# A fused inference step on one core: where finished attention rows are turned, where remainders are formed, and products of constants on TensorE

## The chip, the core and the metric

The kernel runs on one core of one Trainium2 chip. The metric is device microseconds for one execution. Engines are named as in the profile: PE is TensorE, DVE is VectorE, ACT is ScalarE, POOL is GpSimd, SP is SyncE. All of them run at the same time and meet only at semaphores.

## The reference

One layer of a diffusion backbone on 128 context rows and 512 latent rows of width 1024. Cut to what matters here:

```python
sh1, sc1, g1, sh2, sc2, g2 = split(silu(cond) @ w_ada + b_ada, 6)      # two conditions
h = rms_norm(x, norm1_w) * (1 + sc1) + sh1
q, k, v, gu, gv = split(h @ w_in)
q, k = rms_norm per head (8 heads x 64)
a  = attend(q, k, v)      # context: 128 keys; latent: grid neighbourhood + 256 cached keys,
                          # scores + bias, mask, softmax, p @ v
sg = gelu(gu) * (w_s @ layer_norm(gelu(gv)) + b_s)                      # 4 groups x 128
x = x + g1 * (concat(a, sg) @ w_out)
h2 = rms_norm(x, norm2_w) * (1 + sc2) + sh2
x = x + g2 * moe(h2)      # 16 experts, top 1 of 4 groups, top 2 in it
```

Results are y_prompt, y_sample, new_k and new_v, all in fp32.

## The kernel before

The rows are five tiles of 128: tile 0 is context, tiles 1 to 4 are latent. Wherever fp32 accuracy is needed from fast products, a matrix is held as a rounded part in fp32r (hi) and the remainder (lo, "rest"); `three` makes the three products hi·hi, hi·lo, lo·hi.

The stages run in this order: the first modulation (two of six vectors), input projection, spatial gating, attention, output projection with the second norm and the router, then a software pipeline over blocks of 128 gathered rows and an expert's weights, and a gather of the results. All programs are written out by hand, one for each engine, and each engine follows its own program strictly in order.

**Attention** is a list of 40 steps n = (tile, head), eight heads for each tile. At step n PE's program is: scores of step n+1 (`scores`, L1367 for context, L1371 and L1373 for latent); perhaps one part of the second modulation (`ada_part`, L1354); the turn of the probabilities of step n (`prob_T`, L1390, one to five 128x128 transposes into banks 4 and 5); and probabilities times values of step n-1 (`values`, L1412, into bank 6). DVE's `largest` finds the row maximum (L1007 and L1008 for context; L1012, L1016, L1018 for latent, where L1012 adds the bias `bm` in SBUF to the scores in a bank). ACT's `softmax` takes the exponentials, then `copy_pT` (ACT L690, DVE L1028) fetches turned probabilities.

**The second modulation**: two groups of eight parts, at steps 2 to 9 and 20 to 27; each part is four concurrent products of 32x512 outputs into bank 7, with weights that SP streams into a ring of four slots. After a group, `ada_group` on DVE adds the bias from `norms`, and waits for all 14 pieces of the attention bias.

**Finished rows**: once a tile's eight heads are done, DVE's `normalise` (L1042) writes the rows to `o_row`. Two steps later, inside `prob_T`, `att_T` turns them by four transposes (L1419) into bank 4, which is also the bank of the turned probabilities. ACT rounds them (`copy_aT`, L695), DVE forms the rest (`rest_aT`, L984), and PE goes on only after that:

```python
if n >= 2 and steps[n - 2][1] == HEADS - 1:
    att_T(steps[n - 2][0])
    pe.wait_ge(aT_lo_ready, steps[n - 2][0] + 1)
```

**The gating rows** are rounded by ACT (`round_sg`) at steps 2 to 5, and DVE forms their rests (`rest_sg`, L971, L974, L976) at steps 3 to 6, with both inputs in SBUF.

**The attention bias** is made by POOL. After the gating's products it loads `slab`, clears `norms`, issues ten small transfers, and runs 14 additions of 128x512 in SBUF (L521). `largest` of tile 1 waits for 4 of them, of tiles 2 and 3 for 10, of tile 4 for 14.

The output projection starts when all rests are there; its first five tiles of products are L1263 to L1265. Its weights are split by ACT (L622) and DVE (L859) at steps 36 to 40 and behind the loop.

Of the kernel before, what the change touches and what calls it, by code (L numbers as in the profile page):

```python
# [12 lines left out]
ACT = mybir.ActivationFunctionType  # L13
# [39 lines left out]
def build(nc, t_in, t_out):  # L53
# [4 lines left out]
    with ctx:  # L58
# [67 lines left out]

        po, po_r = sb_both("po", 2 * D)
        pT = [po[:, s * 640:(s + 1) * 640].rearrange("p (j n) -> p j n", j=5) for s in range(2)]
        o_row = po[:, 1280:1280 + AW]

        hgT_hi, hgT_lo = [[a.rearrange("p (k n) -> p k n", k=KD) for a in ab] for ab in (
# [3 lines left out]
        rs, rs_r = sb_both("rs", 4 * 512)  # L136
        raw = [rs[:, s * 512:(s + 1) * 512] for s in range(2)]
        sq = [rs[:, (2 + s) * 512:(3 + s) * 512] for s in range(2)]
        y_sb = rs[:, 0:D]
        hidT_hi, hidT_lo = [rs_r[:, D + i * DE:D + (i + 1) * DE].rearrange("p (k n) -> p k n", k=2) for i in range(2)]  # L140
        wr_sb = sb("wr_sb", [P, KD, EXPERTS])
# [157 lines left out]

        ada_first = (2, 20)
        ada_at = {first + k: (g, k) for g, first in enumerate(ada_first) for k in range(KD)}
        ada_ends = {first + KD - 1: g for g, first in enumerate(ada_first)}

# [285 lines left out]
        def _(act):  # L591
# [101 lines left out]
            def copy_aT(t):  # L693
                act.wait_ge(aT_done, t + 1)
                nc.scalar.activation(cat_r[:, 0:4, t * P:(t + 1) * P],  # L695
                                     banks[4][:].rearrange("p (j n) -> p j n", n=P), ACT.Copy).then_inc(aT_copied, 1)

            def round_sg(j):
                if j == 0:
                    act.wait_ge(sgu_out, TILES)  # L700
                row = catT[:, 4 + j, :]
                if j < 3:
                    nc.scalar.activation(rs_r[:, j * TOK:(j + 1) * TOK], row, ACT.Copy).then_inc(sg_hi_ready, 1)
                else:
                    nc.scalar.activation(sg_hi(j, 0), row[:, 0:P], ACT.Copy)
                    nc.scalar.activation(hu_r[:, 56 * P:60 * P], row[:, P:], ACT.Copy).then_inc(sg_hi_ready, 1)

            for n in range(len(steps) + 2):
                if n < len(steps):
                    softmax(n)  # L710
                if 1 <= n <= len(steps):
                    copy_pT(n - 1)
                if n in (2, 3, 4, 5):
                    round_sg(n - 2)
                if 36 <= n < 40:
                    split_hi(("out", 0), n - 36, wout_hi)
                if n >= 2 and steps[n - 2][1] == HEADS - 1:
                    copy_aT(steps[n - 2][0])

            for piece in range(4):  # L720
                split_hi(("out", 1), piece, wout_hi)
# [102 lines left out]
        def _(dve):  # L824
# [143 lines left out]
            def rest_sg(j):  # L968
                dve.wait_ge(sg_hi_ready, j + 1)
                if j < 3:  # L970
                    V.tensor_tensor(cat_r[:, 4 + j, :], catT[:, 4 + j, :], rs_r[:, j * TOK:(j + 1) * TOK].bitcast(F32),  # L971
                                    ALU.subtract).then_inc(sg_lo_ready, 1)
                else:
                    V.tensor_tensor(cat_r[:, 7, 0:P], catT[:, 7, 0:P], sg_hi(3, 0).bitcast(F32),  # L974
                                    ALU.subtract).then_inc(sg_lo_ready, 1)
                    V.tensor_tensor(cat_r[:, 7, P:], catT[:, 7, P:], hu_r[:, 56 * P:60 * P].bitcast(F32),  # L976
                                    ALU.subtract).then_inc(sg_lo_ready, 1)

            def rest_aT(t):
                if t == 0:  # L980
                    dve.wait_ge(bias_ready, 14)
                dve.wait_ge(aT_copied, t + 1)
                ts = slice(t * P, (t + 1) * P)
                V.tensor_tensor(att_lo[:, :, ts], banks[4][:].rearrange("p (j n) -> p j n", n=P),  # L984
                                cat_r[:, 0:4, ts].bitcast(F32), ALU.subtract).then_inc(aT_lo_ready, 1)

            def ada_group(g):
# [43 lines left out]
            def normalise(t):  # L1031
                dve.wait_ge(exp_done, HEADS * (t + 1))
                if t:
                    dve.wait_ge(act_step, HEADS * t)
                    link(V.tensor_tensor(rsum, sums[:, t % 2, :, 0], sums[:, t % 2, :, 1], ALU.add))
                    link(V.reciprocal(rsum, rsum))
                else:
                    link(V.reciprocal(rsum, sums[:, 0, :, 1]))
                dve.wait_ge(pv_done, HEADS * (t + 1))
                if t:  # L1040
                    dve.wait_ge(aT_done, t)
                V.tensor_tensor(o_row.rearrange("p (h d) -> p h d", h=HEADS),  # L1042
                                banks[6][:].rearrange("p (h d) -> p h d", h=HEADS),
                                rsum.unsqueeze(2).to_broadcast((P, HEADS, HD)), ALU.mult).then_inc(o_ready, 1)

            for n in range(len(steps) + 2):
                if n < len(steps):
                    largest(n)
                if 1 <= n <= len(steps):
                    copy_pT(n - 1)  # L1050
                if n - 1 in ada_ends:
                    ada_group(ada_ends[n - 1])
                if n >= 2 and steps[n - 2][1] == HEADS - 1:
                    normalise(steps[n - 2][0])
                    rest_aT(steps[n - 2][0])
                if n in (3, 4, 5, 6):
                    rest_sg(n - 3)
                if 37 <= n < 41:
                    split_lo(("out", 0), n - 37, (wout_hi, n - 36), wout_lo)

            for piece in range(4):
                split_lo(("out", 1), piece, (wout_hi, 5 + piece), wout_lo)
            dve.wait_ge(g1_in, 32)
# [189 lines left out]
        def _(pe):  # L1253
            T = nc.tensor

            def arrived(key):
                slot = slot_of[key]
                pe.wait_ge(ring_in[slot], 16 * nth_of[key])
                return ring[slot]

            def three(out, lhs, rhs, start, stop):

                T.matmul(out, lhs[0], rhs[0], start=start, stop=False)  # L1263
                T.matmul(out, lhs[0], rhs[1], start=False, stop=False)  # L1264
                return T.matmul(out, lhs[1], rhs[0], start=False, stop=stop)  # L1265
# [76 lines left out]
            for t in range(TILES):  # L1342
                if t >= 2:
                    pe.wait_ge(sgu_out, t - 1)
                for g in range(GROUPS):
                    ins = T.matmul(banks[4 + t % 2][:, g * P:(g + 1) * P], vv[:, t, g * P:(g + 1) * P],
                                   wsT[:, g * P:(g + 1) * P], start=True, stop=True)
                ins.then_inc(sgu_done, 1)
            def ada_part(g, k):
                if k == 0 and g:  # L1350
                    pe.wait_ge(rows_ready, g)
                for q in range(4):
                    w = arrived(("ada", 4 + 4 * g + q))
                    ins = T.matmul(banks[7][32 * q:32 * (q + 1), :], silT[:, k, :], w[:, k, :], start=(k == 0),  # L1354
                                   stop=(k == KD - 1))
                if k == KD - 1:
                    ins.then_inc(ada_done, 1)
# [18 lines left out]
            def prob_T(n):  # L1376
                t, h = steps[n]
                pe.wait_ge(exp_done, n + 1)
                if t:
                    pe.wait_ge(act_step, n - HEADS + 1)  # L1380
                if n >= 1:
                    pe.wait_ge(pT_act, n)
                    if dve_copies(n - 1):
                        pe.wait_ge(pT_dve, dve_copies(n - 1))
                if n >= 2 and steps[n - 2][1] == HEADS - 1:
                    att_T(steps[n - 2][0])
                    pe.wait_ge(aT_lo_ready, steps[n - 2][0] + 1)
                for j in range(key_tiles(t)):
                    bank, at_ = (4, j) if j < 3 else (5, j - 3)
                    ins = T.transpose(banks[bank][:, at_ * P:(at_ + 1) * P], probs[n % 2][:, j * P:(j + 1) * P], ident[:])  # L1390
                ins.then_inc(pT_done, 1)
# [23 lines left out]

            def att_T(t):
                pe.wait_ge(o_ready, t + 1)
                for j in range(4):
                    ins = T.transpose(banks[4][:, j * P:(j + 1) * P], o_row[:, j * P:(j + 1) * P], ident[:])  # L1419
                ins.then_inc(aT_done, 1)  # L1420

            pe.wait_ge(cache_in, 64)
# [2 lines left out]
            for n in range(len(steps)):  # L1425
                if n + 1 < len(steps):
                    scores(n + 1)
                if n in ada_at:
                    ada_part(*ada_at[n])
                prob_T(n)  # L1430
                if n:
                    values(n - 1)
            values(len(steps) - 1)
            att_T(TILES - 1)

            pe.wait_ge(exp_done, len(steps))
            pe.wait_ge(aT_lo_ready, TILES)
# [176 lines left out]
```

## Time and profile before

| | us |
|---|---|
| three executions | 817.24, 819.72, 830.25 (median 819.72) |
| the profiled execution | 820.98 |
| its span, first to last instruction | 818.8 |
| PE busy / DVE busy / ACT busy / POOL busy | 640.1 / 436.9 / 309.8 / 146.6 |
| mean granted clock of TensorE | 0.812 |

In a timeline each row is a merged run of like instructions: its start, its length, how many (x), and in brackets how long the engine had been idle and which instruction released it.

### The profile page before, as it was taken

The numbers are of one execution on the slowest core, as the hardware profiler recorded it, in microseconds if no ns is written. First come the engines' busy times: TensorE is split into PE (matmuls) and PEld (weight loads), VectorE is DVE, ScalarE is ACT, GpSimd is POOL, SyncE is SP. The second block draws the span as 40 slices with busy tenths as digits, with TensorE's granted clock in tenths as the row PEclk, the third lists the DMA queues.
The fourth block names the chain that finished last, engine by engine and source line by source line (L and its number), as shares of the span: only waits on it lengthen the run. The fifth ranks groups of instructions, "written<-read, shape, count | busy, mean of one in ns | idle before, by whom it ended". The sixth has DMA issues, their size and how long they took to land. (4 is left out here: it accounts for less than half of the span.)

```text
span 818.8 us, 8534 instructions
## 1 busy us (share of the span) xinstructions
PE 640.1 (78%) x2932; PEld 501.1 (61%) x2932; DVE 436.9 (53%) x634; ACT 309.8 (38%) x500; POOL 146.6 (18%) x175
## 2 busy tenths in 40 slices
PE   3369999988873999999989997049888888888910
PEld 3137888888831577667778776037766766766710
DVE  4227653384338323235442433837777767777628
ACT  5023332220130322244440111326667676766611
POOL 4004220010057000000030000222211122320044
PEclk9568999998955555699559986559999999999965
DMA  9850203564340370005044312086999999998565
GB/s 340 309 204 1 103 14 116 170 228 168 108 154 1 115 296 0 1 1 208 1 168 165 129 51 104 6 341 233 361 335 345 345 353 342 362 353 316 205 219 217
DMA packets 47021, 153.24 MB, mean 187 GB/s; under 512 B 3756, under 2 KB 8892, under 8 KB 39184
## 3 DMA queue, kind: packets, MB, share of 16 engines
q1 hardware_dynamic: 35728, 115.91, 39.1%
q0 software_dynamic: 7392, 25.91, 8.6%
q10 hardware_dynamic: 3872, 11.03, 3.4%
q8 instruction: 18, 0.29, 0.2%
q14 instruction: 11, 0.09, 0.0%
HBM read 131.31 MB, written 21.53 MB: 187 GB/s over the span
## 5 line engine op out<-in xcount | busy, mean ns | idle before, releaser
L1263 PE MATMUL bank<-big_r 128*128 128x512 f32 (+1 forms) x264 | 105.0, 398 | 13.3 <-DVE big_r L859 6.3
L1190 DVE TENSOR_TENSOR big_r<-big,big_r 128x2048 fp32r<-128x2048 f32 x40 | 91.4, 2287 | 29.7 <-ACT big_r L741 29.5
L741 ACT ACTIVATE big_r<-big 128x2048 fp32r<-128x2048 f32 x40 | 76.5, 1915 | 75.5 <-DMA big<-w 74.7
L1264 PE MATMUL bank<-big_r 128*128 128x512 f32 x200 | 82.3, 412 | 0.0
L1263 PEld LDWEIGHTS bank<-big_r 128*128 128x128 f32 x264 | 56.9, 216 | 21.0 <-DVE big_r L859 6.6
L1265 PE MATMUL bank<-big_r 128*128 128x512 f32 (+1 forms) x184 | 67.9, 369 | 0.0
L1265 PE MATMUL bank<-big_r,hu_r 128*128 128x512 f32 x160 | 63.6, 398 | 0.0
L1263 PE MATMUL bank<-hu_r,rs_r 128*128 128x512 f32 x80 | 37.9, 474 | 30.9 <-DVE rs_r L1207 16.8
L1390 PEld LDWEIGHTS bank<-ident,xt 128*128 128x128 f32 x152 | 22.4, 181 | 52.3 <-issue 24.3
L1012 DVE CUSTOM_DVE_ANT_0 xt<-bank,hu 128x256 f32<-128x256 f32 (+1 forms) x32 | 15.7, 490 | 71.4 <-PE bank L1373 71.4
L1390 PE MATMUL bank<-ident,xt 128*128 128x128 f32 x152 | 35.2, 368 | 21.2 <-ACT po L690 14.3
L676 ACT ACTIVATE xt<-xt,small 128x256 f32<-128x256 f32 (+1 forms) x32 | 18.0, 561 | 82.8 <-DVE small L1018 82.8
L1264 PEld LDWEIGHTS bank<-big_r 128*128 128x128 f32 x200 | 44.0, 220 | 7.0
L563 POOL COPY small<-small 128x1 uint32 (+1 forms) x20 | 17.8, 888 | 158.2 <-PE bank L1500 153.7
L1263 PEld LDWEIGHTS bank<-hu_r,rs_r 128*128 128x128 f32 x80 | 17.6, 220 | 42.2 <-DVE rs_r L1207 21.2
L859 DVE TENSOR_TENSOR big_r<-big,big_r 128x1024 fp32r<-128x1024 f32 x28 | 33.3, 1219 | 16.8 <-ACT big_r L622 16.8
L498 POOL TENSOR_TENSOR small<-small 128x8 f32<-128x8 f32 (+1 forms) x15 | 21.5, 1433 | 100.6 <-DVE small L919 60.3
L1265 PEld LDWEIGHTS bank<-big_r 128*128 128x128 f32 x184 | 35.7, 194 | 5.0
L1265 PEld LDWEIGHTS bank<-big_r,hu_r 128*128 128x128 f32 x160 | 34.6, 216 | 5.5
L1500 PE MATMUL bank<-ident,vvr 128*128 128x128 f32 x160 | 22.7, 288 | 19.1 <-DMA vvr<-h_rows,small 12.5
L1263 PE MATMUL bank<-big_r,hu_r 128*128 128x512 f32 x88 | 36.1, 410 | 0.1
L1371 PE MATMUL bank<-qk 64*128 64x256 f32 (+1 forms) x64 | 35.9, 652 | 0.0
(245 smaller groups left out, 1439.9 us busy)
## 6 DMA issues: line engine op xcount, KB each, us to landing
big<-w SPq DMA_DIRECT2D x40, 1024.0 KB, 7.2
big<-w_ada SPq DMA_DIRECT2D x12, 2048.0 KB, 14.6
big<-w_in SPq DMA_DIRECT2D x5, 2048.0 KB, 8.3
cc<-w SPq DMA_DIRECT2D x10, 1024.0 KB, 7.8
xt<-w SPq DMA_DIRECT2D x10, 1024.0 KB
slot_out<-rs ACTq DMA_DIRECT2D x20, 512.0 KB, 5.3
slot_out<-zero SPq DMA_DIRECT2D x1, 5120.0 KB, 22.7
big<-w_out SPq DMA_DIRECT2D x2, 2048.0 KB, 11.1
```

The source lines that it names most:

```text
L498: nc.gpsimd.tensor_tensor(rsq[i % 2][:, 0:w], msq[i % 2][:, 0:w], mhalf[:, 0:w], ALU.pow).then_inc(norm_rstd_ready, 1)
L563: nc.gpsimd.tensor_copy(idx1[p], gidx[:, bass.ds(b, 1)]).then_inc(idx_ready, 1)
L676: nc.scalar.activation(probs[n % 2][:, 0:w], win[n % 2][:, 0:w], ACT.Exp, bias=nmax[:, n % 2:n % 2 + 1], accum_out=sums[:, t % 2, h, 0:1]) ...
L741: nc.scalar.activation(w13_hi[p][:, v, :], w13_raw[v], ACT.Copy).then_inc(w13_hi_ready, 1)
L859: V.tensor_tensor(ring_r[slot][:, ks, :], ring[slot][:, ks, :], ring_r[hi_slot[key]][:, ks, :].bitcast(F32), ALU.subtract).then_inc(ready, 1)
L1190: V.tensor_tensor(w13_lo[p][:, v, :], w13_raw[v], w13_hi[p][:, v, :].bitcast(F32), ALU.subtract).then_inc(w13_lo_ready, 1)
L1263: T.matmul(out, lhs[0], rhs[0], start=start, stop=False)
L1264: T.matmul(out, lhs[0], rhs[1], start=False, stop=False)
L1265: return T.matmul(out, lhs[1], rhs[0], start=False, stop=stop)
L1371: T.matmul(banks[bank][:, 0:nt * P], q, kT[lo:lo + HD, hp, (1 + first) * P:(1 + first + nt) * P], start=True, stop=True)
L1390: ins = T.transpose(banks[bank][:, at_ * P:(at_ + 1) * P], probs[n % 2][:, j * P:(j + 1) * P], ident[:])
L1500: ins = T.transpose(banks[4 + k // 4][:, (k % 4) * P:(k % 4 + 1) * P], hrow[:, k, :], ident[:])
```

## The change

- `att_T` no longer stands in `prob_T`. The turns of tiles 0 to 3 go to steps 14, 18, 30 and 34 of PE's program, ahead of that step's `prob_T`, and into bank 7, which the two groups of the modulation leave free there. The wait for the rest behind the turn is gone; `att_T` waits for `rows_ready` and for the rest of the tile before, and group 1 of the modulation for the rests of tiles 0 and 1.
- `copy_aT` goes to the end of the same steps on ACT; `rest_aT` on DVE stands one step later, behind `largest`.
- The rows of tile 0 are kept in `rs` (`o_rows[0]`), the others in `po` as before.
- `round_sg` goes to steps 16 to 19 and `rest_sg` to steps 17 to 20.
- `keep_busy` is new: a plain fp32 product of the identity and a tile of ones. One stands behind each tile of the gating's products (256 columns, for the last tile 512) and one of 512 behind them all; one of 512 at steps 0, 1, 16 and 32; four of 256 behind the last turn, ahead of the output projection. Nothing reads their results.

```diff
-        o_row = po[:, 1280:1280 + AW]
+        o_rows = [po[:, 1280:1280 + AW]] * TILES
+        o_rows[0] = rs[:, 0:AW]
+        turn_at = {14: 0, 18: 1, 30: 2, 34: 3}
+        busy_at = {0: 0, 1: 0, 16: 1, 32: 3}
 # ACT
             def copy_aT(t):
-                                     banks[4][:]...
+                                     banks[7][:]...
             def round_sg(j):
                 if j == 0:
                     act.wait_ge(sgu_out, TILES)
+                    act.wait_ge(aT_done, 1)
...
-                if n in (2, 3, 4, 5):
-                    round_sg(n - 2)
+                if n in (16, 17, 18, 19):
+                    round_sg(n - 16)
-                if n >= 2 and steps[n - 2][1] == HEADS - 1:
-                    copy_aT(steps[n - 2][0])
+                if n in turn_at:
+                    copy_aT(turn_at[n])
+            copy_aT(TILES - 1)
 # DVE
                 if n < len(steps):
                     largest(n)
+                if n - 1 in turn_at:
+                    rest_aT(turn_at[n - 1])
...
                     normalise(steps[n - 2][0])
-                    rest_aT(steps[n - 2][0])
-                if n in (3, 4, 5, 6):
-                    rest_sg(n - 3)
+                if n in (17, 18, 19, 20):
+                    rest_sg(n - 17)
...
+            rest_aT(TILES - 1)
 # PE
+            def keep_busy(out):
+                T.matmul(out, ident[:], ones[:].unsqueeze(1).to_broadcast((P, out.shape[1] // P, P)), start=True, stop=True)
...
                 ins.then_inc(sgu_done, 1)
+                keep_busy(banks[7][:, 0:256] if t < TILES - 1 else banks[7][:])
+            keep_busy(banks[7][:])
             def ada_part(g, k):
                 if k == 0 and g:
                     pe.wait_ge(rows_ready, g)
+                    pe.wait_ge(aT_lo_ready, 2)
...
-                if n >= 2 and steps[n - 2][1] == HEADS - 1:
-                    att_T(steps[n - 2][0])
-                    pe.wait_ge(aT_lo_ready, steps[n - 2][0] + 1)
...
             def att_T(t):
                 pe.wait_ge(o_ready, t + 1)
+                pe.wait_ge(rows_ready, 1 if t < 2 else 2)
+                if t:
+                    pe.wait_ge(aT_lo_ready, t)
                 for j in range(4):
-                    ins = T.transpose(banks[4][:, j * P:(j + 1) * P], o_row[:, j * P:(j + 1) * P], ident[:])
+                    ins = T.transpose(banks[7][:, j * P:(j + 1) * P], o_rows[t][:, j * P:(j + 1) * P], ident[:])
...
                 if n in ada_at:
                     ada_part(*ada_at[n])
+                if n in busy_at:
+                    if busy_at[n]:
+                        pe.wait_ge(aT_lo_ready, busy_at[n])
+                    keep_busy(banks[7][:])
+                if n in turn_at:
+                    att_T(turn_at[n])
                 prob_T(n)
...
             att_T(TILES - 1)
+            for _ in range(4):
+                keep_busy(banks[5][:, 256:512])
```

## Rows read from the trace of the kernel before

**Rows 1.** Windows of the attention: busy time by engine, granted clock, DMA share, GB/s.

```profile
234.30:249.40 15.10, 15.10 (x54) 5.38 (x54) 8.69 (x7) 3.71 (x11) 14.71 (x17) 0.50 0.02 3
...
279.20:282.60 3.40, 2.03 (x15) 1.91 (x16) 2.38 (x7) 1.65 (x6) 0.00 (x0) 1.00 0.88 285
282.60:340.70 58.10, 56.69 (x194) 41.88 (x192) 16.89 (x59) 17.27 (x57) 0.00 (x0) 0.50 0.35 129
340.70:391.90 51.20, 48.16 (x318) 33.50 (x318) 23.22 (x76) 20.74 (x68) 0.00 (x0) 1.00 0.23 84
391.90:426.00 34.10, 31.67 (x113) 25.62 (x112) 16.70 (x38) 17.13 (x37) 6.83 (x13) 0.50 0.16 54
```

**Rows 2.** Timeline of all engines, steps 2 to 6.

```profile
234.27 1.92 PE L1354 MATMUL bank<-big,norms 128*32 128x512 f32 x2 [1.36 <-DMA big<-w_ada]
...
241.06 20.64 POOL L521 TENSOR_TENSOR hu<-vvr,ada_s 128x512 f32<-128x512 f32 x14
241.31 0.15 DVE L1008 TENSOR_SCALAR small<-small 128x1 f32<-128x1 f32 x1
```

**Rows 3.** DVE's line 971: lengths min/median/max in ns, first and last start.

```profile
L971 DVE TENSOR_TENSOR big_r<-big,rs_r x3: 825/826/19128, 236.6 to 243.3; 128x640 fp32r<-128x640 f32 x3
```

**Rows 4.** Timeline of PE, the turns of steps 4 to 11 and tile 0's.

```profile
242.75 0.48 PE L1390 MATMUL bank<-ident,xt 128*128 128x128 f32 x1
...
246.06 0.48 PE L1390 MATMUL bank<-ident,xt 128*128 128x128 f32 x1
...
263.58 0.45 PE L1390 MATMUL bank<-ident,xt 128*128 128x128 f32 x1 [14.14 <-ACT po L690]
...
272.74 1.12 PE L1390 MATMUL bank<-ident,xt 128*128 128x128 f32 x4
...
276.11 1.94 PE L1354 MATMUL bank<-big,norms 128*32 128x512 f32 x8
277.97 1.12 PE L1419 MATMUL bank<-ident,po 128*128 128x128 f32 x4
280.57 0.66 PE L1390 MATMUL bank<-ident,xt 128*128 128x128 f32 x4 [1.48 <-DVE vvr_r L984]
...
283.43 1.12 PE L1390 MATMUL bank<-ident,xt 128*128 128x128 f32 x4
...
288.08 1.11 PE L1390 MATMUL bank<-ident,xt 128*128 128x128 f32 x4
```

**Rows 5.** The same, tile 1's turn and steps 17, 18, 28 and 29.

```profile
317.45 1.11 PE L1419 MATMUL bank<-ident,po 128*128 128x128 f32 x4
319.98 1.33 PE L1390 MATMUL bank<-ident,xt 128*128 128x128 f32 x5 [1.41 <-DVE vvr_r L984]
...
325.69 1.33 PE L1390 MATMUL bank<-ident,xt 128*128 128x128 f32 x5
...
373.05 0.77 PE L1390 MATMUL bank<-ident,xt 128*128 128x128 f32 x5
...
376.14 0.74 PE L1390 MATMUL bank<-ident,xt 128*128 128x128 f32 x5
```

**Rows 6.** The same, from step 32 to the output projection.

```profile
385.02 0.66 PE L1390 MATMUL bank<-ident,xt 128*128 128x128 f32 x4
...
387.81 0.63 PE L1419 MATMUL bank<-ident,po 128*128 128x128 f32 x4
389.86 0.66 PE L1390 MATMUL bank<-ident,xt 128*128 128x128 f32 x4 [1.41 <-DVE vvr_r L984]
...
411.35 1.11 PE L1390 MATMUL bank<-ident,xt 128*128 128x128 f32 x4
...
417.52 1.06 PE L1412 MATMUL bank<-cc,po 128*128 128x64 f32 x4
419.42 1.12 PE L1419 MATMUL bank<-ident,po 128*128 128x128 f32 x4 [0.84 <-DVE po L1042]
422.00 0.76 PE L1263 MATMUL bank<-big_r 128*128 128x512 f32 x1 [1.46 <-issue]
```

More of the change, by code:

```diff
@@ L695, in copy_aT @@
                 nc.scalar.activation(cat_r[:, 0:4, t * P:(t + 1) * P],
-                                     banks[4][:].rearrange("p (j n) -> p j n", n=P), ACT.Copy).then_inc(aT_copied, 1)
+                                     banks[7][:].rearrange("p (j n) -> p j n", n=P), ACT.Copy).then_inc(aT_copied, 1)
             def round_sg(j):
@@ L983, in rest_aT @@
                 ts = slice(t * P, (t + 1) * P)
-                V.tensor_tensor(att_lo[:, :, ts], banks[4][:].rearrange("p (j n) -> p j n", n=P),
+                V.tensor_tensor(att_lo[:, :, ts], banks[7][:].rearrange("p (j n) -> p j n", n=P),
                                 cat_r[:, 0:4, ts].bitcast(F32), ALU.subtract).then_inc(aT_lo_ready, 1)
@@ L1041, in normalise @@
                     dve.wait_ge(aT_done, t)
-                V.tensor_tensor(o_row.rearrange("p (h d) -> p h d", h=HEADS),
+                V.tensor_tensor(o_rows[t].rearrange("p (h d) -> p h d", h=HEADS),
                                 banks[6][:].rearrange("p (h d) -> p h d", h=HEADS),
```

## The prediction

> **What bounds the kernel now.** I read the page's first part, then the slices of its second part, then windows cut where the granted clock changes, and last the timeline of PE through the attention. TensorE is busy for most of the span, but not at one speed. The windows show the attention in pieces of 1.00 and pieces of 0.50: half speed up to 279.2, 3.4 us at full speed, half again for 58.1 us, full for 51.2 us, half for the last 34.1 us [rows 1]. In the half-speed pieces PE is busy nearly all the time (56.69 of 58.10 us), DVE and ACT under a third of it [rows 1]. So there PE's own clock sets the pace, and a step costs 4.65 us with 256 window columns (288.08 - 283.43) [rows 4] and 5.71 us with 384 (325.69 - 319.98) [rows 5]. At full speed the same steps cost 2.79 us (387.81 - 385.02) [rows 6] and 3.09 us (376.14 - 373.05) [rows 5]. A microsecond saved on PE here comes back at the end, since the output projection, the router and the expert pipeline all start behind it; nothing later waits for a clock of its own.
>
> Two things break PE's work. First, one long hole: step 5's turn starts at 246.06, step 6's at 263.58, 17.52 us later, where steps 4 and 5 lie 3.31 us apart [rows 4]. The end of it is written down to ACT, but ACT waits for DVE's maximum, and DVE sits in a single subtraction at L971 of 19.128 us; its two fellows took 0.825 us [rows 3]. It starts 2.2 us after POOL began its 14 additions (241.06, 20.64 us) [rows 2], and it ends with them. Second, the turns of finished rows: from the turn to the next `prob_T` PE loses 2.60 us for tile 0 [rows 4], 2.53 for tile 1 [rows 5], 2.05 for tile 3 [rows 6], tile 2 like tile 3; the idle part of these is written down to DVE's rest.
>
> The clock is tied to these. It fell in the middle of step 10, 2 us after tile 0's turn was waited for, and again 2 us after tile 3's [rows 1, 4, 6]. It rose at 279.2 and 340.7, both times when a part of the modulation and a run of transposes stood back to back, and in none of the stretches with scores and values alone, though PE was busy all through [rows 1].
>
> **The hole.** With `rest_sg` at steps 17 to 20, nothing of DVE at steps 3 to 7 reads SBUF twice: `largest` of context reads a bank and one small column, and one such ran in 0.15 us at 241.31 beside POOL's additions [rows 2]. So steps 6 and 7 follow at their own pace and the whole 17.52 - 3.31 = 14.2 us goes. What is late next is the attention bias: step 8 needs four of the 14 additions, which are done at 241.06 + 4 x 1.47 = 247, and step 8's turn comes at 272.74 - 14.2 = 258.5; `ada_group` of step 10 waits for all 14, done at 261.7, and comes at about 266. Both are in time. The unknown is L1012, which reads one bank and the bias in SBUF: no row shows it beside POOL's additions. Bounds: free like L1008, or stuck like L971 until 261.7; then step 8's turn comes about where the hole ended, near 263.9, 5.4 us later. I take free, because the second input of L971 is what distinguishes it.
>
> On this the Trainium skill has a rule ("SBUF — State Buffer", section "Who interferes with whom"): a DVE instruction with two SBUF inputs contends with a GpSimd instruction that reads SBUF, one with at most one SBUF input does not. The 19.128 us agree with its first half [rows 3]; by its second half L1012 is free and the sum stands, without it the sum would be 799.
>
> The moved rests and roundings (four instructions on ACT, five on DVE, near 0.83 us for 640 columns) land in steps of 5.71 us in which DVE and ACT are mostly idle [rows 1, 3, 5]. I cost them at nothing; at full speed the cover shrinks to 3.09 us and they could cost some tenths each.
>
> **The turns.** Saved: 2.60 + 2.53 + 2.05 + 2.05 = 9.2 us. Still to be done at the new places: four transposes each, 1.12 us at half and 0.63 at full speed [rows 4, 6], two tiles of each: 3.5 us. The rows of tile 0 now wait for step 14 in a buffer of their own, so nobody waits for them. `copy_aT` now stands ahead of the next `softmax` on ACT and `rest_aT` ahead of a `copy_pT` on DVE; both fall into the time in which ACT and DVE wait for scores. But the fast stretch at 279.2 hung on tile 0's turn standing right behind a part of the modulation. Without it step 10 costs 4.65 instead of 283.43 - 280.57 = 2.86 us: 1.8 us lost [rows 4].
>
> **Products of constants.** The nearest row for one of 512 columns is a part of the modulation, four concurrent plain fp32 products of as many columns: 277.97 - 276.11 = 1.86 us at half [rows 4], so 0.93 at full speed and half of that for 256 columns. Behind the gating they lie in PE's waits for DVE. Those at steps 0 and 1 are hidden by the transfer that step 2 waits for: it lands at 234.27 whatever PE does [rows 2]. That wait also undoes them, I think: PE will now reach it sooner and idle some 3 us, and I expect the clock at 0.50 from there as before. Bounds of this group: 0 and a loss of 1 us if a gating product comes late; a gain of 1 us if the clock holds over the last product of step 2. I take 0. Step 16 costs 1.86, step 32 0.93: 2.8 us. The four behind the last turn cost 4 x 0.47 = 1.9 us where PE idles 1.46 us anyway [rows 6]: 0.4 us at full speed, 2.3 us at half.
>
> **The end of the attention.** With tile 3's wait gone I expect no second fall at 391.9. The work between the last part of the modulation (step 27) and step 33 held the full clock before [rows 1], and steps 34 to 39 are the same work. From step 33's turn to step 38's it took 411.35 - 389.86 = 21.49 us [rows 6]; five steps at 2.79 are 13.95: 7.5 us saved. From there to tile 4's turn (419.42) it took 8.07 us; PE's part halves, the waits for ACT's copies do not: some 2.0 us, and 0.5 for the turn. The output projection's products then start at 1.00 instead of waiting until 426.0 for it: 4.0 us of them take 2.0 [rows 1, 6].
>
> **The sum.** 14.2 + 9.2 - 3.5 - 1.8 - 2.8 + 7.5 + 2.5 - 0.4 + 2.0 = 26.9 us saved. Against the profiled execution's own 820.98 us (span 818.8 and 2.2 around it) this gives 794.1. That execution lies 1.3 us above the median of the three, which is nothing beside their spread of 13 us. I say 794.
>
> **Rivals.** *The clock rises early.* The product of step 16 stands ahead of five transposes, just as parts of the modulation did in both rises. If it lifts the clock, steps 17 to 20 gain 4 x 2.62 and the part in step 20 0.93: 783. If steps 8 or 9 lift it (a part and then four transposes), six more steps gain 1.86 each and the product 0.93: 771. Against it: eight parts of the first group ran at half speed and only one lifted the clock [rows 1, 4]. Chance 0.25. The Trainium skill speaks against it ("TensorE: Matmul & The Clock Gate", section "Part 4: PE-mode transpose"): transposes don't count as busy work in the same way, by which the product alone would not do and 794 would stay; the rise behind tile 0's turn leans the other way [rows 1, 4].
>
> *The end stays slow.* If the clock falls at step 30 or later all the same, 7.5 + 2.5 + 2.0 are not saved and the four products cost 1.9 more: 13.9 us, 808. For it: little PE work fills such a step, and ACT and DVE get the split of the output weights at steps 36 to 40. Chance 0.15.
>
> *The second rise is late, or L1012 is stuck.* Step 20 lifted the clock at once before; the others show that this was luck. Each step later costs 2.62 + 0.93 = 3.55 us. One to four steps late, or one and the 5.4 us of L1012: 798 to 808. Chance 0.14.
>
> *Slower: group 1 of the modulation never lifts the clock*, because its steps now fall at other moments. Then steps 21 to 27 cost 7 x 3.55, 28 to 31 4 x 2.62, 32 and 33 2 x 1.86 more, 39 us, and the end 13.9: 847. It decides from the eighth step missed, when 26.9 / 3.55 = 7.6 steps have eaten the gain. Against it are eight tries. Chance 0.06.
>
> **How the numbers follow.** The forecast itself, 794 give or take 5, has 0.40. The range reaches from the early rise, 769, to the late one and the slow end, 811; outside lie the slower case and some hundredths of extremes. Measurement can tell about 2%, 16.4 us, from no change: below 803.3 lie the forecast, the early rise and a third of the late one, 0.70; above 836 the slower case, 0.06; between them 0.24.
>
> **What would show it.** Right: L971 at 0.83 us three times; no idle PE beyond some us between 234 and 264; step 8's turn near 258; no idle time released by L984 inside the loop; granted clock 1.00 from the early 330s or sooner to the output projection, which starts near 395. Wrong: L1012 of many us beside POOL; 0.50 lasting beyond step 24; a fall of the clock between steps 30 and 39; a new wait of PE at steps 8 or 11 released by POOL or DVE's `ada_group`.

## The result

| | before | changed |
|---|---|---|
| median, us (range, executions) | 820.88 (817.24 to 830.25, 4) | 766.41 (759.85 to 775.43, 4) |
| the profiled execution | 820.98 | 771.05 |
| its span, mean granted clock | 818.8, 0.812 | 768.7, 0.866 |

The changed kernel is faster: ratio 0.9332, 95% interval 0.9232 to 0.9433. It saved 54 us where 26.9 were forecast. 766.41 lies 2.6 us below the range, nearest to the rival "the clock rises early" (771). Of 21 further executions of the kernel before, beside the experiments, three took only 797.27 to 799.63 us, at a mean granted clock of 0.837 to 0.844, and the others, one of 1391.41 us left aside, 813.42 to 846.63 at 0.783 to 0.829: against the three short ones the saving is some 32 us, not 54.

The slices of the granted clock come first, from the second part of the profile's page of the changed kernel (one slice is 19.2 us):

```profile
PEclk9668999998996699998998765699998999999955
```

The attention ends in the nineteenth slice. Windows of the changed kernel, cut where the clock changes (start:end and length, then PE, PEld, DVE, ACT and POOL busy, clock, DMA share, GB/s):

```profile
235.50:262.80 27.30, 27.30 (x102) 11.65 (x101) 5.83 (x23) 6.88 (x26) 24.43 (x22) 0.50 0.01 2
262.80:358.40 95.60, 93.47 (x605) 68.73 (x604) 53.59 (x170) 51.56 (x159) 0.00 (x0) 1.00 0.37 133
358.40:368.60 10.20, 9.31 (x34) 8.34 (x35) 5.28 (x8) 5.01 (x7) 5.17 (x10) 0.50 0.29 114
368.60:409.60 41.00, 39.36 (x179) 32.34 (x177) 14.50 (x20) 3.85 (x6) 3.14 (x11) 1.00 0.52 203
```

Where before had 3.4 us at 1.00 and then 58.1 at 0.50 [rows 1], there is now one stretch of 95.6 us at 1.00. PE is as busy in it as it was at half speed (93.47 of 95.6 us against 56.69 of 58.1); it only gets through more. The next 10.2 us, to just behind the start of the output projection, are slow again.

The instruction of which one took 19.13 us [rows 3] is short all three times at its new place, behind the end of POOL's additions (lengths min/median/max in ns, first and last start):

```profile
L978 DVE TENSOR_TENSOR big_r<-big,rs_r x3: 815/816/816, 284.4 to 290.2; 128x640 fp32r<-128x640 f32 x3
```

The timeline of all engines of the changed kernel, steps 2 to 8:

```profile
233.75 1.05 PE L1371 MATMUL bank<-big,norms 128*32 128x512 f32 x2 [3.19 <-DMA big<-w_ada]
...
239.20 20.74 POOL L526 TENSOR_TENSOR hu<-vvr,ada_s 128x512 f32<-128x512 f32 x14
...
244.11 0.48 PE L1404 MATMUL bank<-ident,xt 128*128 128x128 f32 x1
...
247.43 0.48 PE L1404 MATMUL bank<-ident,xt 128*128 128x128 f32 x1
...
250.37 0.42 DVE L1019 CUSTOM_DVE_ANT_0 xt<-bank,hu 128x256 f32<-128x256 f32 x1 [4.15 <-PE bank L1390]
...
254.95 0.42 DVE L1019 CUSTOM_DVE_ANT_0 xt<-bank,hu 128x256 f32<-128x256 f32 x1 [3.56 <-PE bank L1390]
...
256.61 1.12 PE L1404 MATMUL bank<-ident,xt 128*128 128x128 f32 x4
```

Steps 5 and 6 now lie 3.32 us apart (17.52 before [rows 4]): the hole is gone. The two L1019 (L1012 before) ran beside POOL's additions (239.20 to 259.94) in 0.42 us each. PE waited 3.19 us for weights at step 2, and the clock fell there, at 235.5.

The timeline of PE of the changed kernel, later:

```profile
261.85 1.09 PE L1404 MATMUL bank<-ident,xt 128*128 128x128 f32 x4
...
264.76 0.66 PE L1404 MATMUL bank<-ident,xt 128*128 128x128 f32 x4
...
267.61 0.63 PE L1404 MATMUL bank<-ident,xt 128*128 128x128 f32 x4 [0.29 <-ACT po L695]
...
342.42 0.66 PE L1404 MATMUL bank<-ident,xt 128*128 128x128 f32 x4
...
355.97 0.63 PE L1404 MATMUL bank<-ident,xt 128*128 128x128 f32 x4 [0.29 <-ACT po L695]
...
358.45 1.08 PE L1404 MATMUL bank<-ident,xt 128*128 128x128 f32 x4 [1.01 <-ACT po L695]
...
363.68 1.11 PE L1436 MATMUL bank<-ident,po 128*128 128x128 f32 x4 [0.84 <-DVE po L1049]
364.59 3.62 PE L1272 MATMUL bank<-ones,ident 128*128 128x256 f32 x8
367.65 0.99 PE L1276 MATMUL bank<-big_r 128*128 128x512 f32 x1
```

L1404 is a step's turn of probabilities: 261.85 is step 9's, the next two are steps 10's and 11's, 342.42 is step 33's, 355.97 step 38's, 358.45 step 39's. L1436 is tile 4's turn, the last one, L1272 the four products of constants and L1276 the first product of the output projection. How much earlier each mark stands than before, and what the prediction's terms add up to between the same marks:

| from mark to mark | before | changed | gained | forecast |
|---|---|---|---|---|
| to step 5's turn (246.06) | | 244.11 | 1.9 | 0 |
| to step 6's | 17.52 | 3.32 | 14.2 | 14.2 |
| to step 9's | 16.99 | 14.42 | 2.6 | 2.6 |
| to step 20's (338.99; 295.43) | 58.42 | 33.58 | 24.8 | -3.4 |
| to step 33's | 50.87 | 46.99 | 3.9 | 2.5 |
| to step 38's | 21.49 | 13.55 | 7.9 | 6.9 |
| to the last turn | 8.07 | 7.71 | 0.4 | 2.5 |
| to the output projection | 2.58 | 3.97 | -1.4 | -0.4 |

One row holds the whole surprise: steps 9 to 20, 28 us off. The projection starts 54.4 us earlier and the router ends 54.0 us earlier (511.0, 457.0), but the span is only 50.1 us shorter. The last 4 us went to the expert pipeline (from the router's end on): 307.8 us before, 311.7 now. In the profiles of the twelve experiments below, all with the same pipeline, it took 306.0 to 313.6, so this is its own spread.

### The profile page after: what moved, and what is told of

The parts are those of the page before. It is cut to its first block and busy times, and to the rows that moved or that the text cites. A ratio compares the mean times of both kernels' runs of the same rounds, so it can differ in the third digit from the quotient of the medians.

```text
span 768.7 us, 8596 instructions
## 1 busy us (share of the span) xinstructions
PE 608.2 (79%) x2960; PEld 478.7 (62%) x2960; DVE 417.8 (54%) x634; ACT 309.7 (40%) x500; POOL 146.4 (19%) x175
## 5 line engine op out<-in xcount | busy, mean ns | idle before, releaser
L1276 PE MATMUL bank<-big_r 128*128 128x512 f32 (+1 forms) x264 | 103.9, 394 | 11.9 <-DVE big_r L866 6.3
L1276 PEld LDWEIGHTS bank<-big_r 128*128 128x128 f32 x264 | 56.0, 212 | 18.9 <-DVE big_r L866 6.6
L1276 PE MATMUL bank<-hu_r,rs_r 128*128 128x512 f32 x80 | 38.1, 476 | 33.7 <-DVE rs_r L1216 17.8
L1277 PEld LDWEIGHTS bank<-big_r 128*128 128x128 f32 x200 | 43.5, 217 | 6.7
L1276 PEld LDWEIGHTS bank<-hu_r,rs_r 128*128 128x128 f32 x80 | 17.4, 218 | 44.5 <-DVE rs_r L1216 22.2
L1019 DVE CUSTOM_DVE_ANT_0 xt<-bank,hu 128x256 f32<-128x256 f32 (+1 forms) x32 | 15.7, 491 | 42.3 <-PE bank L1390 42.2
L1278 PEld LDWEIGHTS bank<-big_r 128*128 128x128 f32 x184 | 35.2, 191 | 5.1
L1276 PE MATMUL bank<-big_r,hu_r 128*128 128x512 f32 x88 | 36.1, 410 | 0.1
L1525 PEld LDWEIGHTS bank<-ident,vvr 128*128 128x128 f32 x160 | 22.6, 194 | 21.7 <-DMA vvr<-h_rows,small 12.5
L1278 PE MATMUL bank<-hu_r,rs_r 128*128 128x512 f32 x80 | 35.8, 448 | 0.0
L1404 PEld LDWEIGHTS bank<-ident,xt 128*128 128x128 f32 x152 | 17.7, 148 | 28.7 <-issue 17.5
```

Of the source, the lines that this page charges most:

```text
L1019: V.tensor_tensor_reduce(out=win[p][:, 0:nt * P], in0=banks[bank][:, 0:nt * P], in1=bm[:, h, piece:piece + nt, :].rearrange("p v n -> p (v ...
L1525: ins = T.transpose(banks[4 + k // 4][:, (k % 4) * P:(k % 4 + 1) * P], hrow[:, k, :], ident[:])
```

## The experiments

Two theories of the steps 9 to 20. A: the wait of PE behind a turn is what ends or prevents the full clock, so its price is the half-speed work that follows. B: the turns are worth only their own length, and something else (the closed hole, or the products of constants) lifted the clock. In each expectation A and B are spelled out for that run. The experiments ran in three groups, each on another chip, with seven executions of the kernel before in each: e1 to e4 (median of the kernel before 818.37), e5 to e8 (823.46) and e9 to e12 (817.91).

**Rests alone** (`e1_rests_only`), the kernel before with one edit:

```diff
-                if n in (2, 3, 4, 5):
-                    round_sg(n - 2)
+                if n in (16, 17, 18, 19):
+                    round_sg(n - 16)
...
-                if n in (3, 4, 5, 6):
-                    rest_sg(n - 3)
+                if n in (17, 18, 19, 20):
+                    rest_sg(n - 17)
```

> The kernel before with one part of the change: the gating rows are rounded at steps 16 to 19 and their rests formed at steps 17 to 20; turns and waits as before, no products of constants. Theory A (the hole of 14 us is DVE's line 971 held beside POOL's additions, and its price is its own length): L971 takes 0.83 us three times, the hole is gone, the clock behaves as before, 821 - 14 = 807 us. Rival B (without the hole TensorE never goes cold in front of the latent steps, so most of the gain of the change is in this part): the clock rises at step 9 and mostly stays; under 790 us.

Measured: 809.52 (799.3 to 815.13, 4 executions). Its windows:

```profile
265.30:268.70 3.40, 2.14 (x15) 2.02 (x16) 2.37 (x7) 1.65 (x6) 0.00 (x0) 1.00 0.91 302
268.70:326.70 58.00, 56.59 (x193) 41.78 (x192) 19.84 (x64) 19.80 (x62) 0.00 (x0) 0.50 0.35 128
326.70:377.90 51.20, 48.15 (x318) 33.50 (x318) 23.17 (x76) 20.69 (x68) 0.00 (x0) 1.00 0.24 84
377.90:412.00 34.10, 31.67 (x113) 25.62 (x112) 16.72 (x38) 17.16 (x37) 6.85 (x13) 0.50 0.14 51
```

These are the lengths of before [rows 1], all 14 us earlier, and the profiled execution is 14.6 us shorter (806.39 against 820.98). The medians lie only 8.9 us apart, within the spread of either kernel. A came true: closing the hole is worth the hole and does nothing to the clock.

**Turns alone** (`e2_turns_only`): the changed kernel with roundings and rests of the gating rows back at steps 2 to 6, tile 0's rows back in `po`, and no products of constants (those outside `busy_at` are gone too).

```diff
-        o_rows[0] = rs[:, 0:AW]
...
-            busy_at = {0: 0, 1: 0, 16: 1, 32: 3}
+            busy_at = {}
...
-                if n in (16, 17, 18, 19):
-                    round_sg(n - 16)
+                if n in (2, 3, 4, 5):
+                    round_sg(n - 2)
...
-                if n in (17, 18, 19, 20):
-                    rest_sg(n - 17)
+                if n in (3, 4, 5, 6):
+                    rest_sg(n - 3)
```

> The kernel before with the other part alone: turns of finished rows in bank 7 at steps 14, 18, 30, 34 with their rests one step later; gating rests at steps 3 to 6 as before, no products of constants. Theory A: the hole stays (13 to 15 us), 5.7 us of turns are saved, and the second fall of the clock near the end of the attention is gone (12 us): about 803 us. Rival B (the clock's behaviour hangs on the hole): 0.50 up to step 20 as before and again in the end, 815 us.

Measured: 777.85 (770.22 to 780.84, 4). Both expectations missed, by far. The hole is still there, now ahead of step 5's turn (first row, timeline of PE), yet the clock rises at 270.1, in step 7, and stays (windows):

```profile
261.69 0.45 PE L1400 MATMUL bank<-ident,xt 128*128 128x128 f32 x1 [16.60 <-ACT po L694]
```

```profile
225.70:270.10 44.40, 25.57 (x90) 10.44 (x90) 28.51 (x26) 8.76 (x33) 26.96 (x25) 0.50 0.16 59
270.10:375.90 105.80, 100.92 (x663) 74.16 (x663) 57.11 (x183) 54.89 (x168) 3.03 (x6) 1.00 0.35 124
```

The moved turns alone bring some 40 us between medians. Neither the closed hole nor a product of constants is needed for the long fast stretch.

**No products of constants** (`e3_no_constants`, and the same kernel a second time as `e7_no_constants_again`): the changed kernel with `busy_at = {}` and every `keep_busy` behind the gating and behind the last turn taken out.

> The changed kernel without any product of constants, all else as changed. Theory A (the clock rises at step 9 because a part of the modulation and four transposes stand there back to back, and stays since nothing breaks PE's work; the products are not needed): 763 to 769 us, the clock rises at step 8 or 9. Rival B (the products carry the clock): 0.50 until step 20 or longer, 790 us or more.

> The kernel of e3 again, as the base of the two above and against the changed kernel. Theory A (the products of constants only cost): 758 to 766 us, below the changed kernel's 766 to 772. Rival B (e3 was a lucky draw): 768 us or more.

Measured: 762.23 (760.52 to 768.97, 4) and 760.17 (759.19 to 762.59, 4). Windows of the first:

```profile
227.50:261.60 34.10, 31.29 (x109) 13.36 (x110) 6.18 (x27) 8.31 (x33) 26.07 (x25) 0.50 0.20 74
261.60:364.00 102.40, 97.51 (x642) 72.15 (x641) 58.09 (x182) 55.58 (x167) 3.83 (x7) 1.00 0.36 128
```

The same rise, without them, in step 8, as A had it. In the second profile it rose at 259.2 and fell at 361.6.

**The changed kernel again** (`e4_changed_again`, `e12_changed_third`), beside these.

> The changed kernel itself once more, beside the three others on the same chip. Theory A (the early rise belongs to the kernel): 760 to 775 us and the clock rises at step 8 or 9 again. Rival B (the early rise is chance): this profile shows 0.50 up to step 20 and a time near 790 us.

> The changed kernel a third time, as the base of the three above. Theory A (constants shift the end: the clock falls during steps 38 and 39 and the output projection starts at 0.50): fall at 358 to 360, 766 to 772 us. Rival B (that fall is chance): fall behind 361 us and 760 to 763 us.

Measured: 771.68 (762.1 to 777.48, 4), with rises at 260.4 and 369.6 and a fall at 359.4; and 764.41 (759.3 to 777.22, 4), where the profile has no fall at all before 407.2 (windows, then timeline of PE):

```profile
260.40:407.20 146.80, 142.16 (x847) 108.60 (x846) 75.53 (x203) 62.46 (x176) 8.49 (x21) 1.00 0.41 151
```

```profile
361.57 0.66 PE L1436 MATMUL bank<-ident,po 128*128 128x128 f32 x4 [0.84 <-DVE po L1049]
362.06 1.89 PE L1272 MATMUL bank<-ones,ident 128*128 128x256 f32 x8
```

So the early rise belongs to the kernel, and the fall near 359 comes in some executions and not in others, from one and the same program: A was right for the first and, in kind, B for the second (its 764.41 lies 1.4 us above B's range, and no fall came before 407.2).

What the products of constants cost is not settled. Over three sets and 14 executions the changed kernel averages 767.7, the kernel without them 762.0 over two sets and 8 executions. But most of these 6 us comes from the four longest of the 14 (774.4 to 777.48); the other ten average 764.4, which leaves 2.4 us, with a standard error of 1.8. No gain from them is shown. The version without them has the lowest medians found, clearly below the kernel before and not clearly below the changed one.

**Tile 0's turn back** (`e5_turn0_back`) and **tile 3's** (`e6_turn3_back`), each on the kernel without products of constants: that one tile is turned in `prob_T` in bank 4 again, its rounding (ACT) and its rest (DVE) go back with it, and PE waits for the rest. The part on PE:

```diff
+                if n >= 2 and steps[n - 2][1] == HEADS - 1 and steps[n - 2][0] in turned_old:
+                    att_T(steps[n - 2][0])
+                    pe.wait_ge(aT_lo_ready, steps[n - 2][0] + 1)
```

> The kernel of e3 (changed, no products of constants) with tile 0's turn alone put back to step 9, in bank 4, with PE's wait for its rest. Theory A (the clock rises around step 8 or 9 in every kernel, and what the change removed is the wait of tile 0's turn, which threw it back to 0.50 until step 20): the clock rises near 263, falls within 4 us behind the turn and stays at 0.50 until step 20; 2 us for the wait and some 22 for steps 10 to 20, so 785 to 790 us. Rival B (the wait costs only its own 2 us): 764 us.

> The kernel of e3 with tile 3's turn alone put back to step 33 with its wait. Theory A: the clock falls behind step 33 and stays at 0.50 to the output projection, as in the kernel before: 1.5 us for the wait and 10 to 12 for the end, 773 to 776 us. Rival B: the clock falls near the end of the attention anyway (steps 38 and 39 wait for ACT), so only 2 to 4 us: 765 us.

Measured: 788.95 (785.32 to 797.67, 4) and 777.11 (773.1 to 793.15, 6). Windows of the first, and its timeline of PE:

```profile
229.60:315.00 85.40, 82.03 (x281) 51.28 (x281) 23.61 (x84) 25.32 (x86) 27.07 (x25) 0.50 0.34 123
315.00:383.20 68.20, 66.73 (x441) 48.04 (x441) 37.50 (x117) 35.28 (x111) 0.00 (x0) 1.00 0.18 63
```

```profile
265.51 1.12 PE L1443 MATMUL bank<-ident,rs 128*128 128x128 f32 x4
...
268.11 1.12 PE L1410 MATMUL bank<-ident,xt 128*128 128x128 f32 x4 [1.48 <-DVE vvr_r L994]
...
312.49 1.11 PE L1443 MATMUL bank<-ident,po 128*128 128x128 f32 x4
313.40 1.27 PE L1410 MATMUL bank<-ident,xt 128*128 128x128 f32 x5
314.47 1.03 PE L1432 MATMUL bank<-vr,po 128*128 128x64 f32 x6
```

With the turn and its wait back (1.48 us idle), the rise that all ten profiled executions without this wait have in steps 7 to 9 (the earlier lift below left aside) is absent: half speed for 85.4 us, until step 18. The time is 27 to 29 us above that without it (788.95 against 762.23 and 760.17). The time is as A had it; two details are not: A let the clock rise and fall again there, and it never rose; A let it come back at step 20, and it came at step 18. This run puts the turn and the wait back together, so it does not part them. Against the turn as the cause: in the changed kernel all four moved turns (275.37, 287.94, 332.74, 344.90) lie inside the stretch at 1.00.

For tile 3, the windows behind its wait:

```profile
265.00:347.00 82.00, 79.65 (x519) 57.99 (x519) 43.20 (x141) 40.81 (x129) 0.00 (x0) 1.00 0.43 154
347.00:381.10 34.10, 31.68 (x112) 25.65 (x111) 16.93 (x38) 17.25 (x37) 7.05 (x14) 0.50 0.15 57
```

The clock fell 2 us after step 33's turn (344.83), and the slow end has the 34.1 us of before [rows 1]. The projection starts 13.3 us later than in the kernel without the wait (376.87 against 363.56 in the first profile of it), 12.7 of them behind step 32's turn. A had this right, the time too (1 us above its range).

Not every such wait has this effect. Tile 2's turn in the kernel before is followed by the same wait (timeline of PE of the kernel before):

```profile
359.89 0.66 PE L1419 MATMUL bank<-ident,po 128*128 128x128 f32 x4
361.97 0.77 PE L1390 MATMUL bank<-ident,xt 128*128 128x128 f32 x5 [1.41 <-DVE vvr_r L984]
```

It lies inside the stretch at 1.00 from 340.7 to 391.9 [rows 1], and in that of rests alone likewise (turn at 345.90, next turn of probabilities at 347.97, stretch from 326.7 to 377.9). A part of the modulation stands in each of the steps around it (20 to 27), and none in the steps behind tile 0's and tile 3's turns; that this is the reason is not shown.

**Parts of the constants left out** of the changed kernel: the four at the end (`e8_no_end_constants`), those behind the gating and at steps 0 and 1 (`e9_no_early_constants`), those at steps 16 and 32 (`e10_no_mid_constants`).

> The changed kernel without the four products of 256 columns behind the last turn; the others stay. Theory A (these four run at 0.50 and hold up the output projection, 3.1 us where PE would wait 1.5): 1.5 to 3 us below the changed kernel, and the first output product starts 1.5 us after the turn. Rival B (they pay by lifting the clock for the products behind them): 1 to 2 us above it.

> The changed kernel without the products of constants behind the gating's products and at steps 0 and 1; those of steps 16 and 32 and the last four stay. Theory A (the early ones only hold the clock until PE waits for the weights of step 2, and then it falls anyway): first fall near 228, rise at step 8 or 9, within 3 us of the changed kernel. Rival B (they shift something that matters later): 760 to 763 us, as without any constants.

> The changed kernel without the products at steps 16 and 32; all others stay. Theory A (both run at full speed in PE's path): 2 us less between steps 9 and 33, all else as changed, so 1 to 3 us below the changed kernel. Rival B (they keep the clock from falling in between): a fall between steps 16 and 36 and 775 us or more.

Measured: 772.99 (767.52 to 778.5, 4), 764.61 (760.61 to 768.54, 4) and 775.6 (752.72 to 789.63, 4). None tells what a part of them costs: the first is not below the changed kernel, the second is as A had it but lies in the changed kernel's spread, and the third spreads over 37 us, wider than what it was to tell apart (its profile, of 766.41 us, has no fall between steps 16 and 36, against B). One part of A holds in the first: at the same half speed, the projection starts 2.57 us after the last turn's start (365.04 to 367.61) and not 3.97. And none of them is needed for the rise: it came in all three, at 264.0, 267.3 and 265.8.

**Lifting the clock earlier** (`e11_lift_at_3_and_4`), on the kernel without products of constants:

```diff
+                if n in (3, 4):
+                    for _ in range(2):
+                        keep_busy(banks[5][:, 256:512])
```

> The kernel of e3 with two products of 256 columns more behind the part of the modulation at steps 3 and 4 each, in a free half of bank 5. Theory A (full-height products back to back lift the clock, and then PE runs ahead of POOL's 14 additions, waits 5 us or more around steps 8 to 11, falls to 0.50 and stays there until step 20): rise near 243, fall near 260, 780 to 790 us. Rival B (the wait is too short for a fall, and steps 3 to 11 at full speed pay): 755 to 758 us. Rival C (no lift): 762 to 764 us with the rise at step 8 or 9.

Measured: 782.38 (776.98 to 788.0, 4), 20 us slower than without them, as A had it. Windows, then timeline of PE, then one row of DVE:

```profile
239.20:263.10 23.90, 19.54 (x126) 11.33 (x124) 8.34 (x32) 7.84 (x30) 20.87 (x15) 1.00 0.34 118
263.10:314.30 51.20, 50.78 (x174) 38.00 (x175) 17.87 (x55) 18.31 (x57) 0.00 (x0) 0.50 0.30 110
```

```profile
238.00 1.71 PE L1272 MATMUL bank<-ones,ident 128*128 128x256 f32 x4
...
263.52 0.88 PE L1402 MATMUL bank<-ident,xt 128*128 128x128 f32 x3 [4.78 <-ACT po L695]
```

```profile
260.18 0.69 DVE L1001 TENSOR_TENSOR ada_s<-bank,norms 128x512 f32<-128x512 f32 x1 [5.49 <-POOL hu L526]
```

The clock rose behind these products, 20 us earlier than without them (239.2 against 259.2 and 261.6). PE then ran ahead of the others, reached step 11 too soon and stood idle for 4.78 us. The last row tells why: `ada_group` (L1001), which waits for all of POOL's additions (239.24 to 260.08), held up DVE and with it the next row maximum. The clock fell, and for 51.2 us did not come back.

## Why the prediction was wrong, and where it was right

**The step that failed** is this one: "the fast stretch at 279.2 hung on tile 0's turn standing right behind a part of the modulation. Without it step 10 costs 4.65 instead of 283.43 - 280.57 = 2.86 us". I took the four transposes of the turn for what lifted the clock and the wait behind them for a loss of 2.60 us and no more. The runs show the reverse. With the turn away and everything else of the change undone but the other turns (turns alone), the clock rises in step 7 all the same and stays for 105.8 us. With the turn and its wait put back and nothing else (tile 0 back), it does not rise until step 18. Turn and wait together cost 27 to 29 us, ten times the 2.60 us that the prediction had for them, nearly all of it work at half speed. The prediction had seen that the clock fell 2 us after tile 0's and tile 3's waits and used this for tile 3 (7.5 us) but not for tile 0, because it looked for a cause of the rise there. It also passed over tile 2's wait, as long as tile 3's, behind which the clock did not fall: the trace of the kernel before already showed that a wait alone does not decide.

As a rival it had this outcome (771 for a rise at step 8 or 9) and gave it 0.25, too little: "eight parts of the first group ran at half speed and only one lifted the clock" is no evidence against it, since the parts of steps 2 to 6 lift the clock in none of the kernels that rise in steps 7 to 9. That the profiled execution took 771.05 is in part luck: the rival had 23.5 us more than the forecast for steps 10 to 20, and 28.2 came, while 3.9 us went to the expert pipeline and 3.8 to the tail, the four products and the projection's first ones.

**Right in mechanism and size.** The hole: 14.2 us against 14.2. L1019 beside POOL: 0.42 us against "free". The Trainium skill's rule ("SBUF — State Buffer", section "Who interferes with whom") is that a DVE instruction with two SBUF inputs contends with a GpSimd instruction that reads SBUF, and that one with at most one SBUF input, outside DVE's two-port modes, does not. The trace agrees with both halves (19.13 us before for L971, 0.42 for L1019). The rests at steps 17 to 20: 0.82 us for each of the long ones, at no visible cost. The fall at 235.5 behind the wait for weights. Steps 33 to 38: 7.9 against 6.9 with the turn in it, and tile 3 put back cost 12.7 us from step 32 to the projection: "the end stays slow" without the constants' 1.9 gives 12.0, and its wait less its moved turn 2.05 - 0.63 = 1.4, together 13.4.

**Right in mechanism, off in size.** The products ahead of step 2: taken at 0 and bounded by a gain of 1 us, but step 5's turn came 1.9 us earlier (246.06 - 244.11): the last weights landed 0.5 us sooner (233.75 against 234.27), and the clock held over step 2's work, to 235.5. The tail from step 38 to the last turn: 0.4 us instead of 2.5. It is a chain of ACT's copies and PE's products, with 1.01 us of idle PE in it, and in this execution the clock fell in it at 358.4. The four products: from the last turn to the projection it now takes 3.97 us instead of 2.58 [rows 6], 1.4 us lost where the forecast had 0.4 at full speed and 2.3 at half. In the third profile of the changed kernel, at full speed, the turn ends at 362.23 and the projection starts 1.46 us later (363.69), exactly the idle time of before [rows 6]: there they cost nothing. The first products of the projection: 2.0 us were forecast, and 1.3 came (the projection starts 54.35 us earlier than before, and at the thirteenth product the lead is 426.68 - 371.03 = 55.65 us).

**The Trainium skill's rule on transposes** ("TensorE: Matmul & The Clock Gate", section "Part 4: PE-mode transpose"), that they do not count as busy work in the same way, was weighed against an early rise. It did not help: with tile 0 back, the clock rose at 315.0 behind nine transposes and six products of 64 columns, with no part of the modulation near (ahead of them stand scores of 64 rows and up to 384 columns). So the rule is no ground here to expect no rise; how transposes alone would count, no run here shows.

**Open.** Why the rise comes in steps 7 to 9, and not sooner, wherever tile 0's turn is not waited for. Whether the wait alone, without the turn, keeps it away, and why tile 2's wait does no harm. How often the clock goes another way in the kernel before: its three executions near 798 us, at a mean granted clock of 0.84, would roughly fit if the stretch from 282.6 to 340.7 ran at full speed in them (an estimate: 58.1 us at half speed are 29 at full, and 820.98 - 29 = 792), but no profile of such an execution exists. Whether the products of constants cost 6 us, 2 or nothing: the two in PE's way (steps 16 and 32) took 0.97 and 0.96 us, and the four at the end cost 0 to 1.4. What makes the fall near 359 come in two of three profiled executions of one program.

## What to carry to other kernels

Price a short wait of TensorE not by its length but by the half-speed work that follows until the next rise: here a turn with 1.48 us idle behind it cost 27 us at one place and one with 1.41 cost 13 at another, while 1.41 us idle at a third place, with wide products in every step around it, left the clock up. Look for what stands around each wait. When a clock rises and falls again within microseconds, ask first what ended it, and test the edit that takes the wait away by itself. Run one program several times: here one profile did not decide when the clock falls. Before lifting the clock with products that nothing reads, see where TensorE will run into its next wait: with the waits gone the clock rose without such products, and lifting it too early cost 20 us.

## What the hardware did that was not expected

- The granted clock did not follow from the share of busy time. Steps 10 to 20 ran in 58.0 us at 0.50 with PE busy 56.59 us (rests alone), and in the changed kernel they lay inside 95.6 us at 1.00 with PE busy 93.47.
- A rise can come behind fp32 transposes and products of 64 columns with no part of the modulation near (315.0, tile 0 back).
- One program gave 146.8 us at 1.00 without a break in one execution, and a fall at 358.4 and at 359.4 in two others.
- One DVE subtraction with two SBUF inputs, begun in the midst of POOL's 14 additions, ended 0.7 us after the last of them (243.26 + 19.13 = 262.39 against 261.70): it took 19.13 us against 0.83 [rows 2, 3].
- A wait of 1.41 us left the clock at 1.00 in steps 20 to 27 (before, rests alone) and was followed by a fall 2 us later at step 33.
